# Running the first pair of another feed-forward ahead of its norm, condition rows behind each pair's epilogue, and split tiles through PSUM

## The reference, cut to what matters

```
def adaln(cond, w, b):
    mod = jax.nn.silu(cond) @ w + b
    return jnp.split(mod, 6, axis=-1)

def modulate(xn, shift, scale):
    return xn * (1 + scale) + shift

def swiglu(h, w_gate_up, w_down):
    gu = h @ w_gate_up
    g, u = jnp.split(gu, 2, axis=-1)
    return (jax.nn.silu(g) * u) @ w_down
...
        h = h + g_m * y
        h = h + g_f * swiglu(modulate(rmsnorm_2(h, norm_ffn[i]), sh_f, sc_f),
                             ffn_w_gate_up[i], ffn_w_down[i])
```

## Time and profile before

| What | Value |
|---|---|
| Median of three runs | 1414.39 us (1414.01 to 1415.79) |
| Profiled execution, its time | 1411.35 us |
| Profiled execution, its span | 1409.5 us |
| Mean granted PE clock | 0.989 |
| PE busy | 1372.6 us (97%) |
| DVE busy | 756.1 us (54%) |
| ACT busy | 622.7 us (44%) |
| POOL busy | 851.3 us (60%) |
| Moved by DMA | 227.30 MB, mean 161 GB/s |

### The profile page before, as it was taken

The page is one execution under the profiler, slowest core; times in us unless marked ns, Lnnn a source line. Parts: engine busy times, 40 slices in busy tenths (PEclk is TensorE's granted clock), DMA queues, the critical chain, the costliest instruction groups (busy, mean ns, idle before and its releaser), DMA issues.

```text
span 1409.5 us, 24836 instructions
## 1 busy us (share of the span) xinstructions
PE 1372.6 (97%) x8756; PEld 1219.9 (87%) x8756; DVE 756.1 (54%) x1363; ACT 622.7 (44%) x1011; POOL 851.3 (60%) x424
## 2 busy tenths in 40 slices
PE   9999999999999998899999999999999999999998
PEld 8999999999988886787888888888888788888897
DVE  5987557655544457537555555332524385744411
ACT  6476444445534454524223223222331266655552
POOL 6866888898376466223445444544365442789995
PEclk9999999999999998999999999999999999999999
DMA  7734778894322211113655556553393101455563
GB/s 284 254 137 160 257 269 323 274 330 149 104 96 76 90 61 60 54 67 134 221 179 180 204 189 216 172 184 129 79 258 108 45 1 61 160 186 190 192 211 105
DMA packets 83149, 227.30 MB, mean 161 GB/s; under 512 B 23824, under 2 KB 29200, under 8 KB 82832
## 3 DMA queue, kind: packets, MB, share of 16 engines
q1 hardware_dynamic: 82640, 224.91, 46.8%
q10 hardware_dynamic: 448, 1.57, 0.5%
HBM read 222.26 MB, written 1.05 MB: 158 GB/s over the span
## 4 chain that ended last, share of the span: by engine, by line
PE 45%; issue 29%; POOL 21%; DVE 3%; ACT 1%; DMA 1%; POOLq 0%; SPq 0%; DVEq 0%; ACTq 0%
POOL wl L591 18%; PE ps L1230 8%; PE ps L1232 8%; PE ps L1231 8%; PE ps L1236 5%; PE ps L1237 3%; PE ps L1735 2%; PE ps L1727 1%; PE ps L1329 1%; PE ps L1330 1%; PE ps L1331 1%; PE ps L1749 1%; PE ps L1360 1%; PE ps L1656 1%; DVE xu L1850 1%
## 5 line engine op out<-in xcount | busy, mean ns | idle before, releaser
L591 POOL TENSOR_TENSOR wl<-raw,wh 128x1024 fp32r<-128x1024 f32 x310 | 748.5, 2436 | 489.3 <-ACT wh L701 488.7
L1230 PE MATMUL ps<-xhl,wh 128*128 128x256 f32 (+1 forms) x1344 | 448.4, 334 | 7.0 <-POOL wl L591 2.5
L1232 PE MATMUL ps<-xhl,wl 128*128 128x256 f32 (+1 forms) x1344 | 442.3, 329 | 0.0
L1231 PE MATMUL ps<-xhl,wh 128*128 128x256 f32 (+1 forms) x1344 | 442.1, 329 | 0.0
L701 ACT ACTIVATE wh<-raw 128x1024 fp32r<-128x1024 f32 x310 | 321.7, 1055 | 264.5 <-PE ps L1232 173.6
L1230 PEld LDWEIGHTS ps<-xhl,wh 128*128 128x128 f32 x1344 | 255.9, 190 | 38.2 <-POOL wl L591 5.7
L1232 PEld LDWEIGHTS ps<-xhl,wl 128*128 128x128 f32 x1344 | 256.0, 190 | 23.2
L1231 PEld LDWEIGHTS ps<-xhl,wh 128*128 128x128 f32 x1344 | 256.2, 191 | 21.6
L1230 PE MATMUL ps<-fh,wh 128*128 128x256 f32 (+1 forms) x528 | 168.5, 319 | 0.7 <-POOL wl L591 0.7
L1231 PE MATMUL ps<-fl,wh 128*128 128x256 f32 (+1 forms) x528 | 168.2, 319 | 0.0
L1232 PE MATMUL ps<-fh,wl 128*128 128x256 f32 (+1 forms) x528 | 168.2, 319 | 0.0
(11 more groups left out here) (269 smaller groups left out, 1963.4 us busy)
## 6 DMA issues: line engine op xcount, KB each, us to landing
raw<-wall SPq DMA_DIRECT2D x310, 512.0 KB, 4.0
ada_late<-wada SPq DMA_DIRECT2D x56, 512.0 KB, 3.3
ada<-wada SPq DMA_DIRECT2D x40, 512.0 KB, 5.2
bias<-rpb SPq DMA_DIRECT2D x16, 256.0 KB, 7.4
h<-xin SPq DMA_DIRECT2D x4, 512.0 KB, 5.2
sww<-qk SPq DMA_DIRECT2D x16, 128.0 KB, 2.4
csb<-cond SPq DMA_DIRECT2D x1, 1024.0 KB, 5.4
sw<-u ACTq DMA_DIRECT2D x2, 512.0 KB, 6.4
```

Of the source, the lines that this page charges most:

```text
L591: nc.gpsimd.tensor_tensor(wl[:, slot, :, :], raw[:, slot, :, :], wh[:, slot, :, :].bitcast(F32), ALU.subtract).then_inc(lo_ready, 1)
L1230: nc.tensor.matmul(o, wa, xa, start=start, stop=False, skip_group_check=True)
L1231: nc.tensor.matmul(o, wa, xb, start=False, stop=False, skip_group_check=True)
L1232: return nc.tensor.matmul(o, wb, xa, start=False, stop=stop, skip_group_check=True)
```

## The change

`LED` gets `gu0` too. This makes the existing code of the lead run at the border of `wo0` and `gu0`, 512 tokens wide: splits of h behind each `wo0` pair on ACT and DVE (four instructions each a pair), the `high` of units 2 and 3 of `gu0` inside `wo0`, 16 groups of matmuls in place of filler, the spread factor kept, and `first_led` for pair 0, with the copy of the condition vectors to PSUM and the rows (0,0) and (0,1) behind it. The rows of a phase in `LED` are worked behind each pair's epilogue. In layer 1 the scaled tile goes to PSUM first (`unscaled_tile`), and the high and low parts are taken from there.

```diff
-LED = ("gu1",)
+LED = ('gu0', 'gu1')
...
+        def unscaled_tile(k):
+
+            return ps[:, 2 + k % 2, 0:SEQ]
...
+                if l:
+                    if p:
+                        act.wait_ge(S("xu_ready"), led_before(l) + 2 * p + 1)
+                    for k in (2 * p, 2 * p + 1):
+                        nc.scalar.activation(unscaled_tile(k), h[:, k, 0:SEQ], ACT.Copy, scale=gsc[:, l, 1, k, 0:1])\
+                            .then_inc(S("xu_scaled"), 1)
                 for k in (2 * p, 2 * p + 1):
...
+                    if l:
+                        act.wait_ge(S("xu_scaled"), k + 1)
+                        ins = nc.scalar.activation(xu[n][:, 0, k, 0, 0:SEQ], unscaled_tile(k), ACT.Copy)
+                    else:
+                        for c in range(2):
+                            ins = nc.scalar.activation(xu[n][:, 0, k, c, 0:SEQ], h[:, k, c * SEQ:c * SEQ + SEQ], ACT.Copy,
+                                                       scale=gsc[:, l, 1, k, c:c + 1])
...
+                    if l:
+                        V.tensor_tensor(xu[n][:, 1, k, 0, 0:SEQ], unscaled_tile(k), xu[n][:, 0, k, 0, 0:SEQ].bitcast(F32),
+                                        ALU.subtract).then_inc(S("xu_ready"), 1)
+                        continue
...
-                        else:
+                        elif ph.name not in LED:
                             condition(ph.name, i, j)
                         dve.wait_ge(S("f_lo"), i * 2 + (f0 + j + 1))
...
                                         ALU.subtract).then_inc(S("f_lo"), 1)
+                        if ph.name in LED:
+                            condition(ph.name, i, j)
```

More of the change, by code:

```diff
@@ L788, in unscaled_high @@
                                          ACT.Copy).then_inc(S("xu_high"), 1)
-                for k in (2 * p, 2 * p + 1):
-                    for c in range(n // SEQ):
-                        ins = nc.scalar.activation(xu[n][:, 0, k, c, 0:SEQ], h[:, k, c * SEQ:c * SEQ + SEQ], ACT.Copy,
-                                                   scale=gsc[:, l, 1, k, c:c + 1])
+                if l:
[4 more added lines that the diff above has]
+                            .then_inc(S("xu_scaled"), 1)
+                for k in (2 * p, 2 * p + 1):
+                    if l:
[5 more added lines that the diff above has]
+                                                       scale=gsc[:, l, 1, k, c:c + 1])
                     ins.then_inc(S("xu_high"), 1)
```

## The result

The changed kernel takes 1525.9 us in the median (1523.68 to 1526.78, four runs), the kernel before 1415.09 us. The ratio is 1.078, 95% interval 1.0763 to 1.0797: 110.8 us slower. Predicted were 1531 us, between 1488 and 1568. The profiled execution has 1523.68 us against 1411.35 before, so the two traces are 112.3 us apart.

The account below looks back on a forecast made before the run. PE was taken to set the pace in `gu0`, 10.88 us a pair. The condition-row ring's +117.2 us, `dn0`'s +3 and layer 1's -3.2 made +117 on 1414.39: 1531 us, range 1488 to 1568.

Parts of the forecast that it names:

- the ring: In `gu0`, epilogue, condition rows, weight loads, `high` and silu wait in a circle: 33.4 us an iteration, PE needs 21.8; chance 0.80.
- leg A: In `gu0`, from the end of `fl` of an even pair to that of the next pair: 18.2 us.
- leg B: In `gu0`, from the end of `fl` of an odd pair to that of the next even one: 15.2 us.
- 19 legs, pair 2 to 21: Ten legs A and nine legs B in `gu0`, summed: 318.8 us.
- start of `dn0`: After `gu0`, the third weight unit of `dn0` stands behind row (10,2), which comes later: +3 us (0 to 5).
- layer 1: In `wo1`, the split from PSUM ends earlier and PE's gap and half-rate stretch go: -3.2 us (0 to -4.1).
- The start: First pairs of `gu0`: late rows delay unit 6, PE stands for 13 us, `fl` of pair 2 ends at 678.6.
- The landing: In each leg, weight unit from issue to its `high`: 5.5 us in leg A, 5.0 in leg B.
- silus 18 and 15 us apart in turn: Sign in `gu0` that the prediction is right; silus 10.9 us apart would show it wrong.
- Low clock of PE: Rival: gaps in `gu0` drop PE to 1.2 GHz and it becomes the bound, 1627 us if it stays low; chance 0.08.
- Start alone: Rival: only the 5.5 us at unit 6 of `gu0` stay, less layer 1's 3.2: 1416 us; chance 0.04.
- Faster: Rival: weight loads in SP's queue do not wait for condition rows, PE's lead lasts: 1403.5 us; chance 0.08.

Follow-up runs that it names:

- rows_behind_alone: Kernel before, with only the condition rows of `gu0` moved behind each pair's epilogue, no lead in layer 0, no PSUM path: 1534.07 us, ratio 1.0842.
- rows_front: Changed kernel with the condition rows of `gu0` ahead of each pair's epilogue again, pair 0's excepted: 1418.25 us, ratio 1.002 to the kernel before.
- loads_first: Changed kernel with weight units sent ahead of condition rows in SP's queue, rows still worked behind each epilogue: 1404.65 us, ratio 0.9919 to the kernel before.
- rows_light: Changed kernel, loading only 512 of 1024 columns of each `gu0` condition row, DVE's instructions at full length: 1511.21 us, ratio 1.0681 to the kernel before.
- loads_first_no_lead: Changed kernel with weights ahead of rows in SP's queue, but without the lead in layer 0: 1412.74 us, ratio 0.9981 to the kernel before.

## Why the prediction was right

The deciding step was the ring, and the runs show it: the move of the rows alone costs as much as the whole change (`rows_behind_alone`), undoing it takes the loss away (`rows_front`), and freeing the units from the rows in the queue does too, with the rows left behind the epilogue (`loads_first`). Its terms, from the changed kernel's timelines:

| step | predicted | measured |
|---|---|---|
| first lead matmul on PE | 626.4 | 626.94 |
| end of `modulate` | 645.9 | 643.29 + 2.46 = 645.75 |
| end of pair 1 on PE | 651.9 | 651.49 + 0.39 = 651.88 |
| first condition row | 653.5 | 652.53 |
| units 6 and 7 leave, land | 667.4, 672.5 | 665.07, 669.81 |
| `fl` of pair 2 ends | 678.6 | 676.17 |
| leg A | 18.2 | 17.26 (pairs 2 to 3), mean of ten 17.86 |
| leg B | 15.2 | 708.23 - 693.43 = 14.8 (pairs 3 to 4), mean of nine 14.81 |
| 19 legs, pair 2 to 21 | 318.8 | 988.04 - 676.17 = 311.9 |
| `fl` of pair 21, later than before | 117.2 | 107.8 |
| start of `dn0` | +3 | +3.3, of which the third unit is 1.2 |
| layer 1 | -3.2 | -3.05 |

**The start.** PE's wait is in its timeline:

```profile
673.34 0.80 PE L1244 MATMUL ps<-xhl,wh 128*128 128x512 f32 x1 [10.59 <-POOL wl L595]
```

10.6 us instead of 13. Each row block and the first landing (4.7 us instead of 5.1) came somewhat sooner; the sum was 2.4 us too late at pair 2.

**The legs.** They were 6.9 us too long in the sum over 19, or 0.36 each. Part by part, in the means:

| part | predicted | measured |
|---|---|---|
| leg A: `fl` to the first unit's issue | 6.6 | 6.3 |
| issue to its `high` | 5.5 | 5.2 |
| two `high` | 2.2 | 2.1 |
| silu to the end of `fl` | 3.9 | 4.2 |
| leg B: `fl` to the second unit's issue | 6.1 | 6.0 |
| issue to its `high` | 5.0 | 4.7 |
| one `high` | 1.0 | 1.0 |
| silu to the end of `fl` | 3.1 | 3.1 |

The landing was 0.3 us too long in both legs, 5.6 of the 6.9 us. In legs A the row block was 0.3 us too long as well, and the epilogue 0.3 us too short; these two cancel, and that they do is luck. `fl` falls under POOL in legs A and takes 1.9 us (0.69 before), and 0.83 in legs B. So the mechanism and its terms stood, and the term that was mis-sized is the landing: in legs A I had taken 5.5, between one transfer of 6.0 and the median of 5.1, and the median would have been the nearer choice. The Trainium skill ("DMA: Bandwidth & Descriptors", "Anatomy of one DMA") gives 2.0 us and the bytes at 436 GB/s, fitted on GpSimd's path, where these loads go through SyncE; that is an estimated 3.2 us for a unit. The median of 4.9 does not agree, and `rows_light` shows that bytes of the neighbours belong in the figure.

One sign was put wrong: silus 18 and 15 us apart in turn. These are the lengths of the legs, from `fl` to `fl`. In an odd pair `fl` ends 4.2 us behind its silu and in an even one 3.1, so the silus themselves stand 16.8 and 15.9 us apart.

**Low clock of PE.** This rival fell as the bound of the loop. Windows of the changed kernel (PEclk, DMA share and GB/s last):

```profile
673.00:676.00 3.00, 2.66 (x6) 0.50 0.00 0
...
692.00:696.00 4.00, 4.00 (x13) 0.63 0.00 0
```

The clock does fall to 0.50 in the long gap and is low again for some us at 692. It did so once in each iteration, in or right behind the long gap (4 to 8 us) that PE has there, and the next 3 to 6 us of its work ran at 1.2 GHz. This is why PE is busy for 76% of the stretch and not for the two thirds that I had given as a sign: 19 pairs at 10.88 us would be 207 us, and PE was busy for 232.6. But no silu in `gu0` from pair 2 on waits for PE; the ring is longer than PE's pair even so, and the half-rate time lies in its slack. Where the ring ends it has a price. PE begins `dn0` at 985.21 behind a gap of 7.8 us, at half rate until 988.4. That start is 108.3 us later than before (876.95), 0.5 more than `fl` is; the half rate makes the first 48 matmuls 1.6 us longer; then PE waits about 1.2 us for the third unit. These are the 3.3 us of the table, and the third unit, to which the sum gave all 3, is 1.2 of them. In `rows_front`, where no slack is left, the same fall costs 1.8 us once. The rule of the Trainium skill that I had weighed ("TensorE: Matmul & The Clock Gate", "HAM oscillation"), that each round starts slow behind its wait, agrees with the rows on the clock; in `gu0` it has no price.

**Start alone.** `rows_front` is close to what this rival described: a gap at unit 6 and no loop cost, 1418 us against its 1416. It is what one gets if the rows stay in front.

**Faster.** The rival named the order of the queue as the point that decides, at 1403.5 us. `loads_first` makes that edit and gives 1404.65. The lead is then worth 8.1 us, against 7.7 worked out from the trace before. In its trace the silu of pair 4 stands at 688.12, 4.15 us earlier than before, and 3.2 us had been lost ahead of the lead, so 7.3 us are seen there.

**Layer 1.** Timeline of DVE in the changed kernel, the split of pair 2 of `wo1`:

```profile
1321.73 0.76 DVE L1864 TENSOR_TENSOR xu<-ps,xu 128x256 fp32r<-128x256 f32 x2 [0.25 <-ACT xu L802]
```

0.76 us for two, where two from SBUF took 5.05 under POOL. From the first gated sum of `wo1` to the last root's reciprocal it is 1515.24 - 1307.40 = 207.84 us, against 1403.03 - 1192.14 = 210.89 before.

**The rest of the sum.** The first gated sum of `wo1` is 115.3 us later than before, of which `gu0` and `dn0` make 111.1, the norm behind them 0.7, and the end of the second attention 2.8; 0.7 is spread. 115.3 - 3.05 is the 112.3 us between the profiles. The last three I had not foreseen, and they made up for 4 of the 9 us by which the ring was overestimated. The 2.8 us are no effect of the change (see the last section), so 112.3 - 2.8 = 109.5 us is the better figure for it, beside 110.8 of the medians and 117 predicted. That the forecast of 1531 us came within 5 us is thus luck in part.

## What to carry to other kernels

When work is moved on one engine, look at what a strictly ordered queue has placed behind the waits for that work: here rows that nobody was in a hurry for sat ahead of weights that PE needed next. Close the circle on paper, add its terms and compare the sum with the pace of the bounding engine; a circle that PE had hidden while it turned once in two pairs set the pace when it had to turn once a pair. The cure is as cheap as the fault: order the queue by when its transfers are needed, give loads whose buffers are free first place, and a lead or other gain that a first trial lost may be there after all.

## What the runs showed of the hardware

The end of the second attention differs in the two profiles with no difference in its program. Windows of the changed kernel, then of the kernel before, from the same instruction on (us, PE busy, PEclk, DMA share, GB/s):

```profile
1292.40:1296.40 4.00, 3.16 (x27) 0.91 0.02 4
1296.40:1300.40 4.00, 3.42 (x17) 0.50 0.00 0
```

```profile
1180.00:1184.00 4.00, 3.16 (x30) 1.00 0.02 4
1184.00:1188.00 4.00, 3.42 (x31) 1.00 0.00 0
```

PE had the same work and the same short gaps ahead (0.84 us twice), but the clock fell to 1.2 GHz in one execution and stayed at 2.4 in the other. The last 16 value products of the attention then took 3.14 us (from 1295.13) where they had taken 1.97 (from 1182.70), and 2.8 us were lost until the clock rose. (The 3.42 us of the second windows are not the same work: 17 matmuls at half rate, 31 at the full one.) The profile of the kernel before is the exception. In those of all nine other kernels of this case the clock is below full at this place (0.50 to 0.73 in the lowest 4 us), and the stretch takes 1.3 to 2.8 us more. What sets it off was not tried and stays open.

`gu1` has two paces as well. Its pairs stood 5.54 us apart in six of the profiles, among them before and changed, and 5.65 in four (`rows_front`, `rows_behind_alone`, `loads_first`, `loads_first_no_lead`), with PE full at a granted clock of 1.00 in both, some 2.5 us over its 22 pairs. There is one profile of each kernel, so whether this belongs to the execution or to the program is open. The executions of the kernel before on one chip vary from 1411.7 to 1419.05 us, and part of that may be of these two kinds.

The third thing is that the landing time of a 512 KB unit is no constant: 4.2 to 5.8 us in the median, with what else leaves near it. I sized that from four kernels and have no rule for it.
